# Sums of squares by matmul, reciprocals by head, and spread loads in a hybrid decoder layer

## The reference

```
h = rmsnorm(x, norm_g);  z = h @ w_in            # columns: q k v r a_low gu gv xq gates
o, s_new = gla_chunked(q * DK**-0.5, k, v, log_a, s0)
o = rmsnorm(o, gla_norm_g)                        # per head, 4 heads of 512
branch_a = o * silu(r)
branch_b = spatial gating of gelu(gu), gelu(gv)
branch_c = memory_attention(xq, mem_k, mem_v)     # keys and values: rmsnorm(mem) @ w_mem_kv
merged = g0*(branch_a @ w_br_gla) + g1*(branch_b @ w_br_gmlp) + g2*(branch_c @ w_br_xattn)
x = x + merged @ w_out
x = x + peer_ffn(rmsnorm(x))                      # 8 heads, top 16 of 16384 experts
y = rmsnorm(x)
```

## Time and profile before

| | |
|---|---|
| median of three runs | 4781.91 us |
| profiled execution, own time | 4781.32 us |
| its span in the trace | 4779.6 us |
| granted clock of PE, mean | 0.927 |
| PE busy | 4148.9 us (87%) |
| DVE busy | 3137.7 us (66%) |
| ACT busy | 868.6 us (18%) |
| POOL busy | 1348.8 us (28%) |
| DMA | 1519.45 MB, mean 318 GB/s |

### The profile page before, as it was taken

How to read it: one execution, slowest core, us unless ns; L and a number is a source line. 1 busy time by engine, 2 the same in 40 slices (tenths; PEclk the granted TensorE clock), 3 DMA queues, 4 the chain that set the end, 5 groups by cost and what they waited for, 6 DMA issues and landing times.

```text
span 4779.6 us, 61890 instructions
## 1 busy us (share of the span) xinstructions
PE 4148.9 (87%) x23816; PEld 3602.3 (75%) x23816; DVE 3137.7 (66%) x4574; ACT 868.6 (18%) x1257; POOL 1348.8 (28%) x822
## 2 busy tenths in 40 slices
PE   7999999999788999999866797999999999577555
PEld 7999999999687987887755586887788778344222
DVE  7443134443745656877679876788898655688776
ACT  4334234423322332011000000000000000000000
POOL 0000000000000002432334534444445440466665
PEclk9999999999898999999987798999999999788777
DMA  5555468775354548997999899999999993999998
GB/s 217 195 204 189 142 222 296 286 276 181 101 220 153 219 159 354 415 389 301 408 400 373 320 423 413 423 423 423 423 403 423 423 405 135 386 402 393 422 421 357
DMA packets 304840, 1519.45 MB, mean 318 GB/s; under 512 B 36570, under 2 KB 111786, under 8 KB 138196
## 3 DMA queue, kind: packets, MB, share of 16 engines
q0 software_dynamic: 114288, 830.54, 42.2%
q1 hardware_dynamic: 190356, 686.34, 38.0%
HBM read 1439.05 MB, written 77.71 MB: 317 GB/s over the span
## 4 chain that ended last, share of the span: by engine, by line
PE 49%; DMA 27%; DVE 10%; issue 6%; DVEq 3%; POOL 3%; ACT 2%; SPq 0%; ACTq 0%; POOLq 0%
PE psum L551 28%; DMA sb_raw<-in_wstream 13%; PE psum L3126 9%; DMA sb_ring<-in_peer_v,sb_idx_all 9%; PE psum L605 5%; DMA sb_ring<-in_peer_u,sb_idx_all 4%; POOL sb_ring L2941 2%; DVE sb_acc L2967 2%; DVE sb_ring L2962 2%; PE psum L3368 1%; DVE sb_acc_b L3269 1%; DVEq L2273 1%; PE psum L3350 1%; DVE sb_split L535 1%; POOL sb_ring L2852 1%
## 5 line engine op out<-in xcount | busy, mean ns | idle before, releaser
L551 PE MATMUL psum<-sb_actr,sb_split 128*128 128x264 f32 x8112 | 1015.4, 287 | 41.2 <-DVE sb_split L535 17.8
L551 PEld LDWEIGHTS psum<-sb_actr,sb_split 128*128 128x128 f32 x8112 | 1004.8, 191 | 47.3 <-issue 34.3
L535 DVE TENSOR_TENSOR sb_split<-sb_raw,sb_split 128x2048 fp32r<-128x2048 f32 x201 | 460.6, 2292 | 726.4 <-ACT sb_split L531 724.7
L2852 POOL DMA_INDIRECT sb_ring<-in_peer_u,sb_idx_all x256 | 420.6, 1643 | 1205.1 <-DVEq L2995 584.2
L2962 DVE CUSTOM_DVE_ANT_0 sb_ring<-sb_ring,sb_htok 128x2048 f32<-128x2048 f32 x264 | 597.0, 2289 | 177.5 <-DMA sb_ring<-in_peer_u,sb_idx_all 161.6
L2967 DVE SCALAR_TENSOR_TENSOR sb_acc<-sb_ring,sb_coef,sb_acc 128x2048 f32<-128x2048 f32 x256 | 601.8, 2351 | 134.8 <-DMA sb_ring<-in_peer_v,sb_idx_all 119.3
L2852 POOL DMA_INDIRECT sb_ring<-in_peer_v,sb_idx_all x256 | 458.2, 1790 | 581.6 <-DVE sb_acc L2967 487.0
L3368 PE MATMUL psum<-sb_ring,sb_diag 128*128 128x512 f32 x512 | 346.0, 839 | 239.9 <-DMA sb_ring<-in_peer_v,sb_idx_all 232.6
L3269 DVE SCALAR_TENSOR_TENSOR sb_acc_b<-sb_ring,sb_coef_b,sb_acc_b 128x2048 f32<-128x2048 f32 x192 | 451.2, 2350 | 130.1 <-DMA sb_ring<-in_peer_v,sb_idx_all 116.9
L2941 POOL DMA_INDIRECT sb_ring<-in_peer_v,sb_idx_all x256 | 432.0, 1688 | 301.4 <-DVE sb_acc_b L3269 134.5
L3126 PE MATMUL psum<-sb_h2b,sb_raw_u 128*128 128x256 f32 x2048 | 455.1, 381 | 22.0 <-DMA sb_raw_u<-in_wstream 20.1
(11 more groups left out here) (437 smaller groups left out, 4115.7 us busy)
## 6 DMA issues: line engine op xcount, KB each, us to landing
sb_raw<-in_wstream SPq DMA_DIRECT2D x386, 1024.0 KB
sb_raw_u<-in_wstream SPq DMA_DIRECT2D x64, 1024.0 KB
sb_states<-in_state SPq DMA_DIRECT2D x32, 512.0 KB, 3.7
sb_states_t<-in_stateT SPq DMA_DIRECT2D x32, 512.0 KB, 4.1
out_gla_s<-sb_states SPq DMA_DIRECT2D x32, 512.0 KB, 3.1
dram_z<-sb_zst SPq DMA_DIRECT2D x121, 132.0 KB
dram_z_b<-sb_zst SPq DMA_DIRECT2D x77, 128.0 KB
sb_vrow<-dram_v SPq DMA_DIRECT2D x8, 1024.0 KB, 5.1
```

What stands on the lines that cost most here:

```text
L535: nc.vector.tensor_tensor(split[:, slot, 1, :], raw[:, slot, :], split[:, slot, 0, :], ALU.subtract).then_inc(lo_ready, 1)
L551: last = nc.tensor.matmul(psum[:, bank, 0:ntok], w[a], acts(b, kt), start=(i == 0 and a == 0 and b == 0), stop=(i == len(kts) - 1 and a == 1))
L2852: nc.gpsimd.indirect_dma_start(ring[g % RING][:], None, ins[table], bass.IndirectOffsetOnAxis(ap=col, axis=0)) \
```

## The change

1. The low parts of `actb` leave round 15 of the memory blocks. One is made before the split that precedes block 57's, one before the next stage, two before the gv stage, each ahead of a `split_lo`. Block 14 is evicted right after block 13. PE's first two projection blocks wait for the evictions three blocks back instead of one.
2. ACT copies the first half of the samples' values when the gv stage begins, and the second half first of all when the r stage begins, ahead of Abs, Exp and Ln.
3. In the GLA of group A, DVE's sum over feature tiles is gone. PE sums with sixteen matmuls of 128 columns instead of one of 512. The reciprocal is made by heads inside `normed_heads`: whole for chunk 0, in four parts for chunk 1.
4. DVE's six state updates are made inside the merge's first block, after its `split_lo`. The first two blocks of that loop are written out on DVE.
5. SP issues the state store and `xq` after four merge blocks instead of two, and `kvt` in two halves, four and eight blocks later. The waits on counts follow.

```diff
 def act_samples_start(act):
+    act_samples_values(act, 1)
     act.wait_ge(gx_ready, 1)
...
-    act.wait_ge(rows_turned, 1)
-    for b in range(4):
-        last = nc.scalar.activation(v8[:, b * 512:(b + 1) * 512], psum[0:TS, 6 + b % 2, :], ACT.Copy)
-        if b == 1:
-            last.then_inc(rows_tok, 1)
-            act.wait_ge(rows_turned, 2)
-    last.then_inc(rows_tok, 1)
...
+def act_samples_values(act, half):
+    act.wait_ge(rows_turned, half + 1)
+    for b in (2 * half, 2 * half + 1):
+        last = nc.scalar.activation(v8[:, b * 512:(b + 1) * 512], psum[0:TS, 6 + b % 2, :], ACT.Copy)
+    last.then_inc(rows_tok, 1)
...
 def act_project(act):
...
+                if n0 == N_GV:
+                    act_samples_values(act, 0)
...
-            if n == 15:
-                for k in range(4):
-                    dve.wait_ge(act_hi, 9 + k)
-                    q = slice(4 * k, 4 * k + 4)
-                    nc.vector.tensor_tensor(actb[1][:, q, :], hxb[:, q, :], actb[0][:, q, :], ALU.subtract).then_inc(act_lo, 1)
+        def dve_low_b(dve, k):
+            dve.wait_ge(act_hi, 9 + k)
+            q = slice(4 * k, 4 * k + 4)
+            nc.vector.tensor_tensor(actb[1][:, q, :], hxb[:, q, :], actb[0][:, q, :], ALU.subtract).then_inc(act_lo, 1)
...
+                    for k in range(4):
+                        if n0 == (N_LOW, N_GU, N_GV, N_GV)[k]:
+                            dve_low_b(dve, k)
...
 def pe_project(pe):
...
-                    pe.wait_ge(evac_done, n - 1)
+                    pe.wait_ge(evac_done, n - lag)
...
+                    for n in (n0, n0 + 1):
+                        body(n, n % 2, None, lag=3)
+                    n0 += 2
...
 def pe_sums(pe, c):
-    pe.wait_ge(sums_ready, 6 + c)
-    nc.tensor.matmul(psum[:, 4 + 3 * c, :], ones[:], norm_a[:].rearrange("p h t -> p (h t)"), start=True,
-                     stop=True).then_inc(o_summed, 1)
+    pe.wait_ge(squares_ready, SQUARES_GLA + c + 2)
+    for h in range(HEADS):
+        for j in range(4):
+            last = nc.tensor.matmul(psum[:, 4 + 3 * c, h * CH:(h + 1) * CH], ones[:], sqv[:, 4 * h + j, :],
+                                    start=(j == 0), stop=(j == 3))
+    last.then_inc(o_summed, 1)
...
 def dve_gla(dve):
...
-            def squares_summed(c):
-                dve.wait_ge(squares_ready, SQUARES_GLA + c + 2)
-                nc.vector.tensor_reduce(norm_a[:], sqv[:].rearrange("p (h j) t -> p h t j", h=HEADS), AX.X,
-                                        ALU.add).then_inc(sums_ready, 1)
...
-                nc.vector.reciprocal(norm_a[:], norm_a[:])
-                dve.drain()
...
             def normed_heads(c, h0, h1):
...
+                nc.vector.reciprocal(norm_a[:, h0:h1], norm_a[:, h0:h1])
+                dve.drain()
...
-            sp_merge(sp, N_BA, N_BA + 2)
+            sp_merge(sp, N_BA, N_BA + 4)
             sp_state(sp)
             sp_attention_first(sp, GA)
-            sp_merge(sp, N_BA + 2, N_BC)
+            for k in range(2):
+                sp_merge(sp, N_BA + 4 + 4 * k, N_BA + 8 + 4 * k)
+                sp.dma_start(kvt[:, 8 * k:8 * k + 8, :], mem_dram[:, 8 * k:8 * k + 8, :]).then_inc(kvt_loaded, 16)
+            sp_merge(sp, N_BA + 12, N_BC)
...
-            state_update(dve, 2, 8)
-            dve_merge(dve, N_BA, N_BC, True)
+            dve_merge(dve, N_BA, N_BC, True, beside=lambda: state_update(dve, 2, 8))
```

More of the change, by code:

```diff
@@ L1987, in sp_attention_first @@
             sp.dma_start(xq[:], src).then_inc(xq_loaded, 16)
-            if g.samples:
-                sp.dma_start(kvt[:], mem_dram).then_inc(kvt_loaded, 16)
-            else:
+            if not g.samples:
                 sp.dma_start(kvt[:, 0:8, :], mem_dram[:, 0:8, :]).then_inc(kvt_loaded, 16)
@@ L2208, in piece @@
                     dve_piece(dve, merged, 16, k // 2 - 1)
+            if beside is not None:
+                for n in (n0, n0 + 1):
+                    body(n, n % 2, None, [(n, n % 2, 0, n - n0, 0 if n == n0 else (n - N_BA) // 2)], beside if n == n0 else None)
+                n0 += 2
             merge_loop(dve, n0, n1, body, piece if n0 == N_BB else None)
@@ L2632, in pe_out @@
             wide_loop(pe, N_OUT + 2, N_WQ, body)
-            pe_spread(pe, 8, WA)
+            pe_spread(pe, 6, WA)
             for u in range(3):
```

27 lines of the change are left out of this document (13 added, 14 removed).

## The result

The changed kernel took 4750.75 us (median of 4 runs, 4746.84 to 4755.33) against 4782.2 for the kernel before in the same comparison: ratio 0.9935, 95% interval 0.9918 to 0.9952. Two more comparisons gave 0.9946 (0.9930 to 0.9963) and 0.9943 (0.9928 to 0.9958). Over all comparisons the kernel before ran 74 times, median 4781.2, from 4769.5 to 4792.1, and the changed one 14 times, median 4750.8, from 4746.1 to 4762.6. The medians differ by 30.4 us and the means by 29.2, with a standard error of about 1.3 (the standard deviations are 4.8 and 4.3). A ratio given here is the comparison's own estimate and can differ by 0.001, some 5 us, from the quotient of the two medians beside it.

A forecast was written before the change was run, and what follows sets the result against it. PE, busy 87% of the span, was taken as the bound: its work plus its gaps. Terms 0.8 + 5.5 - 0.5 + 5.3 + 5.9 = 17.0 us took 4781.3 to 4764.3, forecast as 4765; range 4755 to 4775.

The forecast's parts named there:

- A: Memory blocks to projections: block 16 starts 5.1 us sooner, block 17 follows a new gap; gain 0.8 us, bounds -0.5 and 2.8.
- B: Samples' values at blocks 73 and 74: PE's wait for ACT's copies goes; gain 5.5 us, bounds 4 and 6.
- C: GLA of group A, sums on PE and reciprocals by heads, up to block 137: -0.5 us, bounds -4 and +2.
- D: State updates beside block 137: PE's idle time before block 138 and its half clock go; gain 5.3 us, bounds 3.5 and 5.6.
- E: Loads for attention: the 6.98 us gap goes, a 2.1 us stall before block 144 stays; gain 5.9 us, bounds 3 and 8.8.
- given back later: Rival, behind the edited places: a later gap covered by chance, or other clock falls, eat most gain; 4779 us, chance 0.08.

The follow-up runs named there:

- D alone: Kernel before with only the six state updates moved beside the first merge blocks, behind the next block's low part: 4774.71 us, ratio 0.9993.
- B alone: Kernel before with only two of the samples' four copies made eight blocks earlier: 4771.16 us, ratio 0.9985.
- the change without C: Changed kernel with the sums of squares on DVE again and reciprocals in one piece: 4756.38 us, ratio 0.9941; again 4756.76, 0.9947.
- the last kernel: Changed kernel with block 17's operands before the last memory eviction, xq and kvt's first half spaced out, samples' loads one block later: 4742.33 us, ratio 0.9913.
- A alone: Kernel before with only group B's four low parts beside later blocks and PE's first two projection blocks asking for fewer evictions: 4774.49 us, ratio 0.9993.
- C alone: Kernel before with only the sums of squares made by PE and the reciprocals by heads: 4780.43 us, ratio 0.9995.
- The drained kernel: Kernel before with eight drains put into DVE's program before the copies of attention, nothing else computed: one time of 4772.45 us.

## Why the prediction was too small

**The terms held.** A: block 16 and block 17 stood where the text put them, gain 0.4 for 0.8; the edit of block 17's operands shows that the wait for the store was the limit. B: 6.1 for 5.5, because block 74 starts 0.7 us late and without a fall. C: -0.6 for -0.5, with both chunks right to 0.1 us; that the sum is so near is in part luck, since the three executions gave -0.8, -0.9 and -0.1. D: 5.3 for 5.3. E: 7.0 for 5.9 (its own sum, 6.98 + 1.8 - 3.0, is 5.8). The stall before block 144 was there with 1.35 to 1.78 us instead of 2.1; the 0.9 us of clock behind it were not. The Trainium skill's rule of ring order ("DMA: Bandwidth & Descriptors", "Queues, rings and completion order") agrees with that stall and with its end once xq is issued later; no run here tells it apart from transfers that share the bandwidth.

**The step that failed** is the last one: "Groups B and the experts keep their instructions, and all of them start behind group A, so I carry the gain to the end in full", and with it the zero that I silently gave to every other stretch of group A. I gave no term to places that the diff does not touch, and took the range from the terms alone. Measured, these places gave 10.2 of the 13.4 us that were missed: 2.1 and 1.7 at blocks 60 and 119, 0.5 behind it, 1.9 in attention, -1.3 in the merges behind it, and 5.3 behind output 216. The terms gave 1.2 more, and 2.0 are in no trace. The argument against the rival "given back later", that the chain "runs through PE with no independent clock of its own", was wrong as well: what lies behind can move by itself, here the other way.

**What is shown of these 10 us.** Block 119 takes 12.6 to 13.2 us in all eight executions with A and 13.5 to 18.2 in all eight without, whatever else they have. So A brings that gain. The longer PE program alone did not (15.46).

The traces show how the block gets late. PE waits there for a low part that DVE makes behind its work on the samples' cache. That work waits for loads that SP issues behind a store (L681) and four cache loads (L822). In each of the sixteen executions a fetch of instructions overlaps one of these issues. In the seven with the short PE program it is the store, which then takes 1.14 to 1.89 us instead of 0.43 to 0.46. In the eight with A it is the third cache load (1.26 to 1.88), and in the kernel before with PE's blocks written out the second (1.60). The last load that DVE needs lands 1.9 to 2.6 us before block 118 ends with A, and at most 1.3 before it in the others. So this is a fetch among SP's issues again; why its place matters so much is open. Timeline rows of SP, kernel before and then the changed one:

```profile
988.61 1.14 SPq L681 DMA_DIRECT2D out_gla_s<-sb_states  x1
992.23 2.00 SPq L822 DMA_DIRECT2D sb_cache<-in_kcache  x4
```

```profile
979.84 0.46 SPq L681 DMA_DIRECT2D out_gla_s<-sb_states  x1
982.75 2.92 SPq L822 DMA_DIRECT2D sb_cache<-in_kcache  x4
```

SP's short issue at 377 comes from PE's longer program. It is 1.30 to 1.68 us in all nine executions that have PE's blocks written out and 2.56 to 2.85 in the seven without, though block 60 follows it only loosely: 8.0 to 11.1 us in the six executions with A and SP's order unchanged, 9.1 to 12.7 without A. (The seventh with A, the one with block 17 early, took 7.7.)

In attention the gain is a fall of the clock that is absent. None came in the three executions of the changed kernel, with D alone and with block 17 early (78.5 to 78.7 us); with B alone it came only behind attention (79.0). In the other ten, the change without C and the last kernel among them, it came and attention took 80.0 to 80.7. So it goes with the kernel and not with one part. With A alone and with C alone it came 18 us later than in the other eight, behind the next gap.

**What stays open.** The 5.3 us behind 216. The five executions with all parts took 2973.2 to 2977.2 us there; the eleven others 2974.5 to 2985.2, with a mean of 2981.1. The ranges touch, and no single part does it: C alone took 2985.2, D alone 2974.5. Less half clock is not the reason: behind 216 PE was at half clock for 558 us in the mean of the three executions of the kernel before and for 565 in those of the changed one. The drained kernel, one of the three counted as before, was the fastest of them there (2975.9); without it the gain would be 7.8. From output 216 to the end of the table stage the five executions with all parts took 2175.8 to 2180.3 us and the eleven others 2179.2 to 2187.5. From there to the end one kernel differs from another by up to 11 us (793.8 to 805.1). I can't say how much of the 5.3 is a cause and how much a draw. Nor is it settled whether leaving out C costs some 5 us, as the pooled times say, or nothing, as the ratios say, when C by its own work costs 0.6.

## What to carry to other kernels

Terms worked out from the gap, the next late operand and the half clock behind it came out within 1.1 us each here, while the half clock itself was the least sure part of them. The method leaves out everything else: with sixteen executions at hand, untouched stretches gave 10 us in sum between two versions. The times of one kernel lay up to 23 us apart, and those of the kernel with A alone 32. Give such stretches a width of their own in the range, in both directions, and don't call a difference of 10 us on a 4.8 ms kernel the effect of an edit before its own place in the trace shows it. When a gap goes, look at what is late next: block 17's operands stood behind an unneeded wait, and two reordered statements there gave as much in the trace as the largest of the five parts.

## What was unexpected about the chip

A DMA issue on SP takes longer when a fetch of 16 KB of instructions falls into it: 2.56 to 2.85 us in seven executions against 1.30 to 1.68 in nine for the same load. The length of another engine's program moves the fetch against the issue: in one experiment PE's alone was changed. Whose instructions the fetch brings is not shown. The Trainium skill ("Runtime: NRT & Kernel Launch", "Instruction fetch mechanics") says that instructions are refilled in blocks of 16 KiB and that this is mostly hidden. The packets have that size here, but some 1.2 us at SP, the difference of the means, are not hidden.

A pause of 0.33 us between two small DVE instructions came and went with where DVE's program lies: the step from one to the next was 0.41 us in the six executions that have neither C nor D nor the drains, and 0.08 in the ten that have one of them. All three change the length of that program. A changes it too and left the pause as it was.

The gap of 1.35 to 1.78 us before block 144 was not followed by half clock in the changed kernel, one of 2.83 us there (in the second execution without C) was. The gap of 1.95 us in attention was followed by it in four executions and not in six, and the one of 2.29 to 2.30 us in four and not in two. So a gap's length alone doesn't tell whether the clock falls.
